# A decoder step on one core: w_down tiles as whole row groups over four banks, and output copies moved behind the next block's high parts

## The reference, cut to what matters

```
h = silu(x @ w_gate[e]) * (x @ w_up[e])        # 2048 -> 512
y += gate[token, e] * (h @ w_down[e])          # 512 -> 2048
```

## Time and profile before

| | |
|---|---|
| median of three runs | 1499.52 us |
| profiled execution | 1501.56 us, its span 1499.7 us |
| PE | 1442.7 us busy, 96% of the span |
| ACT | 774.6 us, 52% |
| DVE | 1014.7 us, 68% |
| POOL | 193.5 us, 13% |
| high parts in the expert stage | L1037, x196, mean 1920 ns |
| low parts in the expert stage | L1659, x196, mean 2292 ns |
| loads of w_down | 68 of 1024 KB |
| DMA in the second half | 370 to 390 GB/s |

### The profile page before, as it was taken

How to read it: one execution, slowest core, us unless ns; L and a number is a source line. 1 busy time by engine, 2 the same in 40 slices (tenths; PEclk the granted TensorE clock), 3 DMA queues, 4 the chain that set the end, 5 groups by cost and what they waited for, 6 DMA issues and landing times.

```text
span 1499.7 us, 24322 instructions
## 1 busy us (share of the span) xinstructions
PE 1442.7 (96%) x9396; PEld 1293.6 (86%) x9396; DVE 1014.7 (68%) x1287; ACT 774.6 (52%) x912; POOL 193.5 (13%) x99
## 2 busy tenths in 40 slices
PE   8999999999999999999997989999999999999994
PEld 7999999999999999999996457888888888888781
DVE  4246746747768787423025668888888888888787
ACT  4245545444443423311110147778778778777774
POOL 0000000000000000324330001211221212212130
PEclk9999999999999999999998899999999999999997
DMA  7321231322213212634335599999999999999997
GB/s 261 122 89 57 85 113 61 111 74 85 103 57 105 109 57 74 203 137 149 133 102 203 200 384 369 382 388 389 390 374 384 388 387 392 387 384 384 351 293 231
DMA packets 89749, 335.36 MB, mean 224 GB/s; under 512 B 12086, under 2 KB 18790, under 8 KB 60874
## 3 DMA queue, kind: packets, MB, share of 16 engines
q1 hardware_dynamic: 84202, 315.54, 56.5%
q0 software_dynamic: 5472, 18.74, 4.9%
HBM read 313.56 MB, written 40.73 MB: 236 GB/s over the span
## 4 chain that ended last, share of the span: by engine, by line
PE 84%; DVE 7%; DMA 4%; ACT 3%; issue 1%; ACTq 0%; SPq 0%; DVEq 0%
PE BANK L1787 13%; PE BANK L1788 13%; PE BANK L1789 13%; PE BANK L2145 6%; PE BANK L2147 6%; PE BANK L2146 6%; PE BANK L2194 4%; PE BANK L2192 4%; PE BANK L2193 4%; DMA RAWB<-in_w_up 3%; PE BANK L2129 2%; PE BANK L2158 2%; PE BANK L1929 1%; PE BANK L1805 1%; DVE LOB L1659 1%
## 5 line engine op out<-in xcount | busy, mean ns | idle before, releaser
L1787 PE MATMUL BANK<-XH,HI 128*128 128x260 f32 x1746 | 503.7, 289 | 1.4 <-DVE RT L1463 1.0
L1659 DVE TENSOR_TENSOR LOB<-RAWB,HIB 128x2048 fp32r<-128x2048 f32 x196 | 448.5, 2292 | 77.1 <-ACT HIB L1037 76.4
L1788 PE MATMUL BANK<-XL,HI 128*128 128x260 f32 x1746 | 496.0, 284 | 0.0
L1789 PE MATMUL BANK<-XH,LO 128*128 128x260 f32 x1746 | 495.2, 284 | 0.0
L1037 ACT ACTIVATE HIB<-RAWB 128x2048 fp32r<-128x2048 f32 x196 | 376.2, 1920 | 104.5 <-PE BANK L2147 64.2
L1787 PEld LDWEIGHTS BANK<-XH,HI 128*128 128x128 f32 x1746 | 332.0, 190 | 2.6 <-issue 1.7
L1788 PEld LDWEIGHTS BANK<-XL,HI 128*128 128x128 f32 x1746 | 331.7, 190 | 0.6
L1789 PEld LDWEIGHTS BANK<-XH,LO 128*128 128x128 f32 x1746 | 331.7, 190 | 0.0
L2145 PE MATMUL BANK<-HIB,XGH 128*128 128x512 f32 x512 | 202.0, 395 | 9.6 <-DVE LOB L1659 5.6
L2147 PE MATMUL BANK<-LOB,XGH 128*128 128x512 f32 x512 | 200.2, 391 | 0.0
L2146 PE MATMUL BANK<-HIB,XGL 128*128 128x512 f32 x512 | 199.8, 390 | 0.0
(11 more groups left out here) (382 smaller groups left out, 1646.0 us busy)
## 6 DMA issues: line engine op xcount, KB each, us to landing
RAWB<-in_w_down SPq DMA_DIRECT2D x68, 1024.0 KB, 11.4
RAWB<-in_w_gate SPq DMA_DIRECT2D x67, 1024.0 KB, 9.8
RAWB<-in_w_up SPq DMA_DIRECT2D x67, 1024.0 KB, 10.8
RAW<-in_w_in SPq DMA_DIRECT2D x39, 1024.0 KB, 5.0
RAW<-in_w_out SPq DMA_DIRECT2D x16, 1024.0 KB, 5.1
Y<-in_xT SPq DMA_DIRECT2D x8, 520.0 KB, 9.3
RT<-in_xT SPq DMA_DIRECT2D x16, 260.0 KB, 5.3
x_rows<-R SPq DMA_DIRECT2D x5, 832.0 KB
```

The costliest lines, as they stand in the source:

```text
L1659: dve.tensor_tensor(LOB[:, s, :], RAWB[:, r, :], HIB[:, s, :].bitcast(F32), ALU.subtract).then_inc(b_lo[s], 1)
L1787: pe.matmul(bank, hw[:, c, :], h, start=(c == 0), stop=False)
L1788: pe.matmul(bank, hw[:, c, :], l, start=False, stop=False)
L1789: ins = pe.matmul(bank, lw[:, c, :], h, start=False, stop=(c == KC - 1))
```

## The change

For all blocks but the last two, a w_down tile becomes a row group: 128 of the 512 rows by all 2048 columns, one run of 8 KB per partition. Its 12 matmuls now go to four banks, three to each, and the four banks are complete only after the fourth tile. The four output copies then come after h_hi and bhi 2 of the next block, one by one, each followed by one of bhi 3 to 6. The last two down products keep column tiles, the last one in four banks of its own. Since down now has banks 2, 4, 5 and 7, the turned tokens take banks 6 and 3 (2 for the very first group), and two waits are added on PE: tokens(0) for the low part of H, and turn_h for the low part of the third token group. POOL's program is not changed.

```diff
+        DOWN_BANK, LAST_DOWN_BANK = (2, 4, 5, 7), (0, 1, 3, 6)
+        def t_bank(g, j):
+            if g % 2:
+                return 3
+            return 2 if isinstance(j, int) and j == 0 else 6
...
# SP
-            def down(j, first):
+            def down(j, first, columns=False):
                 e = sp.value_load(EBI[0:1, bass.ds(j - 1, 1)], min_val=0, max_val=NE - 1)
                 for n in range(4):
-                    w = a["w_down"][bass.ds(e, 1), :, :, 512 * n:512 * n + 512].rearrange("a p c n -> p (a c) n")
+                    if columns:
+                        w, parts = a["w_down"][bass.ds(e, 1), :, :, 512 * n:512 * n + 512].rearrange("a p c n -> p (a c) n"), 4
+                    else:
+                        w, parts = a["w_down"][bass.ds(e, 1), :, n, :].rearrange("a p n -> p a n"), 1
...
-                with sp.If(j < nb):
+                with sp.If(j < nb - 1):
                     gate_up(j, 0)
                     down(j, 8)
-            down(nb, 0)
+            gate_up(nb - 1, 0)
+            down(nb - 1, 8, True)
+            down(nb, 0, True)
# ACT
-            def out_copy(n, i, j, into=YO):
+            def out_copy(n, into=YO, banks=DOWN_BANK):
+                act.activation(into[:, 512 * n:512 * n + 512], BANK[:, banks[n], :], ACT.Copy).then_inc(b_y, 1)
+
+            def column_copy(n, i, j, into=YO, banks=DOWN_BANK):
 
                 act.wait_ge(b_used, 12 * j - 3 + i)
-                act.activation(into[:, 512 * n:512 * n + 512], BANK[:, 4 + n % 2, :], ACT.Copy).then_inc(b_y, 1)
+                out_copy(n, into, banks)
...
+            h_hi(0)
+            for i in range(2, 7):
+                bhi(i, 0, 1)
             with act.Fori(1, MAXB) as j:
                 with act.If(j < last):
-                    h_hi(j - 1)
-                    for i in range(2, 10):
+                    for i in range(7, 10):
                         bhi(i, 0, j)
                     silu(j)
                     token_hi(0, j + 1)
                     bhi(10, 0, j)
-                    act.wait_ge(b_yw, 16 * j)
-                    out_copy(0, 8, j)
                     token_hi(1, j + 1)
                     bhi(11, 0, j)
-                    out_copy(1, 9, j)
                     token_hi(2, j + 1)
                     bhi(0, 0, j + 1)
-                    out_copy(2, 10, j)
                     token_hi(3, j + 1)
                     bhi(1, 0, j + 1)
-                    out_copy(3, 11, j)
+                    h_hi(j)
+                    bhi(2, 0, j + 1)
+                    act.wait_ge(b_yw, 16 * j)
+                    act.wait_ge(b_used, 12 * j + 8)
+                    for n in range(4):
+                        out_copy(n)
+                        bhi(3 + n, 0, j + 1)
...
# PE
                 elif g == 0:
                     pe.wait_ge(b_xg, 16 * j)
+                    pe.wait_ge(b_hl, j - 1)
...
-            def turn_h(j):
+            def turn_h(j, after=None):
                 pe.wait_ge(b_h, j + 1)
                 if not isinstance(j, int):
                     pe.wait_ge(b_hl, j)
+                if after is not None:
+                    pe.wait_ge(b_xl, after)
...
-            def down(n, i, j, th=HTH, tl=HTL):
+            def down(c, i, j, th=HTH, tl=HTL, banks=DOWN_BANK):
+
+                if c == 0:
+                    pe.wait_ge(b_hl, j)
+                    pe.wait_ge(b_y, 4 * (j - 1) + 2)
+                hw, lw = ready(i, 0, j)
+                for n in range(4):
+                    b = BANK[:, banks[n], :]
+                    pe.matmul(b, th[:, c, :], hw[:, n, :], start=(c == 0), stop=False)
+                    pe.matmul(b, tl[:, c, :], hw[:, n, :], start=False, stop=False)
+                    ins = pe.matmul(b, th[:, c, :], lw[:, n, :], start=False, stop=(c == 3))
+                ins.then_inc(b_used, 1)
+
+            def down_column(n, i, j, th=HTH, tl=HTL, banks=DOWN_BANK):
...
-            turn_h(0)
+            turn_h(0, 7)
...
-                    turn_h(j)
+                    turn_h(j, 4 * j + 7)
             gate_up(last, 0)
             for n in range(4):
-                down(n, 8 + n, last)
+                down_column(n, 8 + n, last)
...
-                down(n, n, nb, HTH2, HTL2)
+                down_column(n, n, nb, HTH2, HTL2, LAST_DOWN_BANK)
```

More of the change, by code:

```diff
@@ L670, in down @@
                     passed(sp)
-                    sp.dma_start(RAWB[:, s, :].rearrange("p (c n) -> p c n", c=4), w).then_inc(b_raw[s], 16)
+                    sp.dma_start(RAWB[:, s, :].rearrange("p (c n) -> p c n", c=parts), w).then_inc(b_raw[s], 16)
             gate_up(1, 0)
@@ L1050, in token_hi @@
                 act.wait_ge(b_tx, 4 * j + g + 1)
-                act.activation(XGH[:, 4 * g:4 * g + 4, :], BANK[:, 2 + g % 2, :].rearrange("p (c n) -> p c n", c=4), ACT.Copy).then_inc(b_xh, 1)
+                act.activation(XGH[:, 4 * g:4 * g + 4, :], BANK[:, t_bank(g, j), :].rearrange("p (c n) -> p c n", c=4), ACT.Copy).then_inc(b_xh, 1)
             def h_hi(j, into=HTH):
@@ L1083, in _ @@
                     bhi(10, 0, j)
-                    act.wait_ge(b_yw, 16 * j)
-                    out_copy(0, 8, j)
                     token_hi(1, j + 1)
                     bhi(11, 0, j)
-                    out_copy(1, 9, j)
                     token_hi(2, j + 1)
                     bhi(0, 0, j + 1)
-                    out_copy(2, 10, j)
                     token_hi(3, j + 1)
                     bhi(1, 0, j + 1)
-                    out_copy(3, 11, j)
-            h_hi(last - 1)
-            for i in range(2, 10):
+                    h_hi(j)
[5 more added lines that the diff above has]
+                        bhi(3 + n, 0, j + 1)
+            for i in range(7, 10):
                 bhi(i, 0, last)
@@ L1100, in _ @@
             act.wait_ge(b_yw, 16 * last)
-            out_copy(0, 8, last)
+            column_copy(0, 8, last)
             bhi(11, 0, last)
-            out_copy(1, 9, last)
+            column_copy(1, 9, last)
             h_hi(last, HTH2)
             bhi(0, 0, nb)
-            out_copy(2, 10, last)
+            column_copy(2, 10, last)
             bhi(1, 0, nb)
-            out_copy(3, 11, last)
+            column_copy(3, 11, last)
             bhi(2, 0, nb)
-            out_copy(0, 0, nb, YO2)
+            column_copy(0, 0, nb, YO2, LAST_DOWN_BANK)
             bhi(3, 0, nb)
             for n in range(1, 3):
-                out_copy(n, n, nb, YO2)
+                column_copy(n, n, nb, YO2, LAST_DOWN_BANK)
             act.activation(MV2[:, 0, 3:4], EPS_LN2, ACT.Sqrt)
-            out_copy(3, 3, nb, YO2)
+            column_copy(3, 3, nb, YO2, LAST_DOWN_BANK)
             def samples_copy(n):
@@ L1668, in token_lo @@
                 dve.wait_ge(b_xh, 4 * j + g + 1)
-                dve.tensor_tensor(XGL[:, 4 * g:4 * g + 4, :], BANK[:, 2 + g % 2, :].rearrange("p (c n) -> p c n", c=4),
+                dve.tensor_tensor(XGL[:, 4 * g:4 * g + 4, :], BANK[:, t_bank(g, j), :].rearrange("p (c n) -> p c n", c=4),
                                   XGH[:, 4 * g:4 * g + 4, :].bitcast(F32), ALU.subtract).then_inc(b_xl, 1)
@@ L2128, in tokens @@
                 for c in range(4):
-                    ins = pe.transpose(BANK[:, 2 + g % 2, 128 * c:128 * c + 128], rows[:, 4 * g + c:D:KC], IDENT[:, :])
+                    ins = pe.transpose(BANK[:, t_bank(g, j), 128 * c:128 * c + 128], rows[:, 4 * g + c:D:KC], IDENT[:, :])
                 ins.then_inc(b_tx, 1)
@@ L2182, in turn_h @@
                 ins.then_inc(b_th, 1)
-            def down(n, i, j, th=HTH, tl=HTL):
+            def down(c, i, j, th=HTH, tl=HTL, banks=DOWN_BANK):
[10 more added lines that the diff above has]
+            def down_column(n, i, j, th=HTH, tl=HTL, banks=DOWN_BANK):
                 if n == 0:
                     pe.wait_ge(b_hl, j)
-                pe.wait_ge(b_y, 4 * (j - 1) + n + 1)
+                    if banks is DOWN_BANK:
+                        pe.wait_ge(b_y, 4 * (j - 1) + 2)
                 hw, lw = ready(i, 0, j)
-                b = BANK[:, 4 + n % 2, :]
+                b = BANK[:, banks[n], :]
                 for c in range(4):
```

## The result

The changed kernel takes 1604.74 us (median of six runs, 1604.12 to 1610.39) against 1498.74 us in the same measurement: a ratio of 1.0711, 95% interval 1.0689 to 1.0734. It is 106 us slower; the forecast was 75 us slower, with 1604 us as the upper end of its range. The profiled execution has a span of 1602.5 us, so the traces show 102.8 us of the difference.

What follows compares the result with a forecast made beforehand. PE, the matmul engine, was taken to set the pace. 14 x (4.2 us wait + 1.2 us clock) = 75.6, + 1 for the end, - 1 for the loads, gave 1575 us against the median of 1499.52; range 1541 to 1604.

Steps and rivals of the forecast that it cites:

- the loop of waits: Late copy 3 delays scatter, then gather; PE waits 4.2 us in 14 periods (S: a block's first gate matmul).
- the edits costed at nothing: Down phase's four banks, PE's added waits for tokens and turn_h, output copies in ACT's idle time: 0 us.
- The relief of the loads: w_down loads in 8 KB runs relieve the DMA engines; between 0 and -5 us, taken as -1.
- The end: After the loop, the last scatter lands later and the quarter scatters may go late: +1 us.
- the landing: Time from the gather's issue to its arrival, now beside gate and up tiles: taken as 9.6 us, between 9.1 and 10.3.
- the clock: PE's granted clock falls after the wait, slowing the down phase: 0 to 1.6 us per period, taken as 1.2.
- The likeliest case: Gather late in each period and clock falling after most gaps: 1575 us, own range 1546 to 1593; chance 0.58.
- the case of the much later gather: Rival: weights squeeze the gather, which lands in 12.0 us; from 1593 up to 1627 us; chance 0.12.

Runs made afterwards that it cites:

- e1: Changed kernel with POOL's order alone altered: the gather issued ahead of the scatter that waits for copy 3; 1497.81 us, ratio 0.9985.
- e3: Kernel before with one wait added on POOL, holding index copy and gather until PE has used the block's fifth gate or up tile; 1592.75 us, ratio 1.0639.
- e5: Kernel before with the same edit as e1, the gather ahead of the scatter on POOL, nothing else; 1497.89 us, ratio 0.9986.
- e6: Changed kernel with w_gate and w_up stored so each tile loads as four 2 KB runs, 8 KB apart in HBM (except block 0); 1566.48 us, ratio 1.0447.
- e9: Changed kernel with the gather ahead of the scatter as in e1, but held until PE has used the fifth gate or up tile; 1564.34 us, ratio 1.0434.
- e2: Changed kernel with 20 unused matmuls of 512 columns added on PE ahead of its wait for the gather; 1584.3 us, ratio 1.0562.
- e7: Changed kernel with the four output copies in two pairs, one behind bhi 2 and one behind bhi 3; 1508.71 us, ratio 1.0068.
- e8: Changed kernel with all four output copies together behind bhi 2; 1509.13 us, ratio 1.0056.

## Why the prediction was right and wrong

**Right: the loop of waits.** That copy 3 is now behind bhi 5, that the scatter and, in POOL's order, the gather hang on it, and that PE's wait is then in every period. Issue of the gather forecast S+16.46, measured S+16.34; 14 periods; the undisturbed period unchanged (e1). e1 and e3 show it from both sides: take the lateness away and all of the loss is gone; put it alone into the kernel before and 93 us appear.

**Right: the edits costed at nothing.** Banks, extra waits of tokens and turn_h, copies in ACT's idle time: e1 has the period of before. The relief of the loads, forecast -1 us, cannot be told from nothing: e1 and e5 are level, though w_down loads land in 7.3 us in e1 and 10.3 in e5. The end, forecast +1: from the last S to the end of the span it is 82.4 us before and 83.6 after. There the size came out right by luck: the last scatter of the loop went at S+13.3 and landed in 10.3 us, not at S+11.8 and in 7.5, so the first quarter scatter went at S+29.4 in place of S+27.1, and of these 2.3 us the end shows 1.2.

**Wrong in size: the landing, 9.6 us.** This is the step that failed first. It was 11.0, so the wait was 5.57 and not 4.2: 14 x 1.4 = 19 us. I had two neighbours, 9.1 beside w_down tiles and 10.3 beside gate and up tiles, and took a value between them, though the gather was to run mainly beside the second kind; and I thought the emptier engines of a longer period would help. e6 shows that the packets beside it are worth 2.0 us. The rule of the Trainium skill that I had weighed (page "DMA: Bandwidth & Descriptors", section "Queues, rings and completion order": turns between queues, packet by packet) pointed the right way. The scatter was rightly taken as equal: it goes 4.6 us ahead of the gather before and after. It is worth 1.8 us in the changed kernel (e9), but it stood as close when the 9.1 us were measured; whether the two effects add up, no run shows.

**Wrong in size: the clock, 1.2 us.** This is the second step that failed. It was 1.96: 14 x 0.76 = 11 us. I had priced one fall as in the earlier trace rows and expected it in most blocks. It came in all 14, and nine of them cost more than the 1.6 us seen before: turns to H turn 14.2 to 15.6 us against 12.87. e2 shows that it was the clock. The two terms feed each other: behind a later landing a fall is also surer, as the list at the end shows.

19 + 11 = 30 us, from 1575 to the 1604.7 measured. Both misses went the same way. The likeliest case was bounded by waits of 5.0 us (a landing of 10.4, the longest in the earlier trace rows) and 1.6 us for the clock, and the means, 5.57 and 1.96 us, both lie beyond these bounds. A single gather of before had run beside gate and up tiles, and its 10.3 us were no bound for such a place. Only the case of the much later gather, to which I gave 0.12, reaches the value; its reason, weights that squeeze the gather, is the one that e6 bears out.

## What to carry to other kernels

When work is moved later on one engine, follow its result through the program order of every engine that waits for it: what stands behind the waiting instruction is late too, even if it needs nothing of the moved work. If it ends in the next turn's start, the delay is paid in every turn. Price a transfer at its new place by its new neighbours, the packets beside it and the transfer just ahead of it, and price an idle PE with the clock it loses: a gap of 5.6 us cost 7.5. Here one reordered gather gives back the whole loss, but what is left is a kernel level with the old one, for the runs of w_down were never on the path.

## What the runs showed of the hardware that I had not expected

**Gaps and the clock.** The 56 periods of the changed kernel, e3, e6 and e9 give a list of PE's waits (how late the turns start against S+21.89) and whether the down phase behind them ran at the lower level (over 14 us) or not (12.97 or less). Nine waits of 1.59 to 2.95 us: no fall. Four of 3.32 to 3.59 us: three falls. The 43 of 3.76 us and more: a fall each time. Yet in the first block of the kernel before two waits of 1.75 and 1.99 us, 5 us apart, brought one; and in e2, behind the 20 added matmuls, one idle stretch of 2.01 us brought a fall (down phase 14.54 us) while one of 2.34 us did not. So the length of the last wait alone does not decide it.

**One gather, many prices.** A gather of the same rows took 9.2, 11.0, 10.35, 9.0 and 9.2 us as mean of 14 in the kernel before, the changed one, e3, e6 and e9, and 10.7 and 10.9 in e7 and e8.
